# Expert weights of a mixture layer: experts taken one at a time, in longer runs, instead of two at a time

## What is computed

```python
# x: (1, 512, 1024); w_e1, w_e3: (16, 1024, 2816); w_e2: (16, 2816, 1024)
def _expert_choice_ffn(x, w_router, w_e1, w_e3, w_e2):
    cap = CAPACITY_FACTOR * n // N_EXPERTS                    # 64
    aff = jax.nn.softmax((x @ w_router).astype(F32), axis=-1)
    gate, idx = lax.top_k(jnp.swapaxes(aff, 1, 2), cap)
    xin = jax.vmap(lambda xb, ib: xb[ib])(x, idx)
    hid = jax.nn.silu(jnp.einsum('becd,edf->becf', xin, w_e1)) * jnp.einsum('becd,edf->becf', xin, w_e3)
    y = jnp.einsum('becf,efd->becd', hid, w_e2) * gate[..., None].astype(x.dtype)
    # y is added back at the token positions idx; then out = LN(alpha * h + sum)
```

## Time and profile before

| what | us |
|---|---|
| time, median of 3 runs | 2093.16 (2092.58 to 2097.62) |
| span of the profiled execution | 2092.3 |
| TensorE matmul busy | 1913.1 (91%) |
| VectorE, ScalarE, GpSimd busy | 649.0, 380.3, 252.2 |
| matmuls at L1078 idle on a transfer of expert weights | 102.1 |

### The profile page before, as it was taken

One profiled execution on the slowest core, in us unless ns is written; L12 is line 12 of the kernel. 1 busy time (PEld: TensorE's weight loads), 2 busy tenths in 40 slices (PEclk: granted clock), 3 DMA queues, 4 the chain that ended last, 5 costly groups with the idle time before them and its releaser, 6 DMA issues.

```text
span 2092.3 us, 20357 instructions
## 1 busy us (share of the span) xinstructions
PE 1913.1 (91%) x8502; PEld 954.8 (46%) x8502; DVE 649.0 (31%) x1149; ACT 380.3 (18%) x691; POOL 252.2 (12%) x268
## 2 busy tenths in 40 slices
PE   8989999999999997999798799898898888888897
PEld 4656554466678754343343343343343334334332
DVE  6599747588865442001001001001000000100102
ACT  1434313189810021000000000000000000000001
POOL 1786500065400000000000000000000000000001
PEclk9999999999999998999899999999999999999999
DMA  5631304143332576999999999999999999999995
GB/s 148 135 96 56 115 13 138 47 148 121 121 141 91 202 328 260 425 426 428 427 426 430 427 427 428 427 426 429 430 423 429 428 426 428 428 425 428 428 426 217
DMA packets 93786, 638.17 MB, mean 305 GB/s; under 512 B 21580, under 2 KB 35328, under 8 KB 62464
## 3 DMA queue, kind: packets, MB, share of 16 engines
q1 hardware_dynamic: 81056, 628.99, 74.0%
q10 hardware_dynamic: 12640, 7.89, 1.3%
HBM read 626.98 MB, written 9.88 MB: 304 GB/s over the span
## 4 chain that ended last, share of the span: by engine, by line
PE 59%; DMA 29%; DVE 2%; ACT 2%; issue 0%; SPq 0%; DVEq 0%
PE ps L1078 58%; DMA arena<-in_w_e 29%; ACT arena L730 1%; ACT L730 0%; PE ps L1189 0%; DVE arena L2191 0%; DVE arena L2148 0%; PE ps L1590 0%; SPq L531 0%; PE ps L1252 0%; PE ps L1306 0%; DVE arena L2185 0%; DVE arena L2092 0%; DVE arena L2094 0%; PE ps L1443 0%
## 5 line engine op out<-in xcount | busy, mean ns | idle before, releaser
L1078 PE MATMUL ps<-arena 128*64 128x512 f32 (+8 forms) x7968 | 1849.9, 515 | 144.4 <-DMA arena<-in_w_e 102.1
L1078 PEld LDWEIGHTS ps<-arena 128*64 128x64 f32 (+2 forms) x7968 | 893.7, 163 | 1077.7 <-issue 957.4
L730 ACT ACTIVATE arena<-ps 128x512 f32<-128x512 f32 (+6 forms) x288 | 155.8, 573 | 1591.2 <-PE ps L1078 903.8
L2157 DVE TENSOR_TENSOR arena<-arena,ps 128x512 f32<-128x512 f32 (+1 forms) x48 | 30.2, 643 | 575.3 <-PE ps L1078 575.3
L722 POOL TENSOR_TENSOR arena<-arena 128x1024 f32<-128x1024 f32 x3 | 7.0, 2349 | 1360.3 <-ACT arena L730 1360.3
L2166 DVE TENSOR_TENSOR arena<-arena,ps 128x512 f32<-128x512 f32 x48 | 33.1, 690 | 334.5 <-PE ps L1078 334.5
L730 ACT ACTIVATE arena<-arena 128x128 f32<-128x128 f32 (+10 forms) x261 | 117.7, 509 | 73.3 <-DVE arena L2116 19.1
L730 ACT ACT_TABLE_LOAD x74 | 94.9, 1283 | 25.5 <-issue 23.8
L1870 DVE SCALAR_TENSOR_TENSOR arena<-arena 128x512 f32<-128x512 f32 x80 | 63.5, 794 | 2.8
L2148 DVE TENSOR_TENSOR arena<-arena 128x512 f32<-128x512 f32 x8 | 5.5, 693 | 180.6 <-PE ps L1590 180.5
L682 POOL TENSOR_TENSOR arena<-arena 128x768 f32<-128x768 f32 x16 | 28.5, 1779 | 179.4 <-PE ps L1252 128.4
(11 more groups left out here) (206 smaller groups left out, 702.5 us busy)
## 6 DMA issues: line engine op xcount, KB each, us to landing
arena<-in_w_e SPq DMA_DIRECT2D x112, 2816.0 KB, 29.2
arena<-in_w_e SPq DMA_DIRECT2D x80, 2048.0 KB, 27.7
arena<-in_w_e SPq DMA_DIRECT2D x32, 1408.0 KB, 11.7
arena<-in_w_in SPq DMA_DIRECT2D x9, 2048.0 KB, 8.6
arena<-in_w_e SPq DMA_DIRECT2D x16, 1024.0 KB, 30.4
arena<-cumulative_scratch SPq DMA_DIRECT2D x16, 768.0 KB, 4.9
arena<-in_w_in SPq DMA_DIRECT2D x5, 1536.0 KB, 6.5
arena<-in_w_out_ssd SPq DMA_DIRECT2D x4, 1536.0 KB, 7.1
```

Source lines behind the costliest of these rows:

```text
L730: return act.activation(out, in_, func, **kw)
L1078: return pe.matmul(out, lhsT, rhs, start=a, stop=z)
L2157: tt(o, o, ps[:, i, 0:w], ALU.mult).then_inc(s.hid_ready, 1)
```

## The change

One expert is taken at a time. The two halves of the array now take the two halves of an expert's 2816 up columns (1408 each, in banks of 512, 512 and 384), and in `down` the two halves of its 1024 output columns; a matmul has the same shape of stationary operand as before. w_e1 accumulates in banks 0 to 2, w_e3 in banks 3 to 5, the output in bank 6. From expert 3 on each weight tensor of an expert comes as two pieces of 11,264 words per partition: four rows of w_e1 or w_e3, or eleven of w_e2, in one run of 45,056 bytes. Experts 0 to 2 and the last piece of expert 15 are cut finer. A piece's landing is told by one of 18 semaphores instead of 12. The loads of the second norm's rows are issued after the copy of expert 0's output. `gates_transposed`, `gather` and `sums_so_far` stand at other places between the products; the gathered columns of `h` are taken with a step of 4 instead of 2, the transposed blocks with a step of 11 instead of 4.

```diff
-BANKS = [(512 * i, min(512, FF - 512 * i)) for i in range(6)]
-ROW_BLOCKS = KT // 2
-BLOCKS = len(BANKS)
-LANDINGS = 12
-BY_ROWS = 2 * ROW_BLOCKS
+HALF_FF = FF // 2
+BANKS = [(512 * i, min(512, HALF_FF - 512 * i)) for i in range(3)]
+RUN = (4, 4, 11)
+ROW_WORDS = (FF, FF, D_MODEL)
+LANDINGS = 18
...
+def expert_pieces():
+    cuts = lambda x, w, j: {
+        (0, 0): [0, 1, 2, 3, 4], (0, 1): [0, 1, 2, 3, 4],
+        (0, 2): [0, 3, 5, 8, 11] if j == 0 else [0, 3, 6, 9, 11],
+        (1, 0): [0, 1, 2, 3, 4], (1, 1): [0, 2, 4], (1, 2): [0, 6, 11], (2, 0): [0, 2, 4], (2, 1): [0, 2, 4],
+        (EXPERTS - 1, 2): [0, 11] if j == 0 else [0, 6, 9, 11]}.get((x, w), [0, RUN[w]])
+    return [(x, w, j, r0, r1) for x in range(EXPERTS) for w in range(3) for j in range(2)
+            for r0, r1 in zip(cuts(x, w, j)[:-1], cuts(x, w, j)[1:])]
...
-        aside = {piece_at[0, 0]: hid_at, piece_at[ASIDE, 0]: aside_at, piece_at[ASIDE, 1]: aside_at + FF}
+        aside = {piece_of[0, 0, 1, 3]: hid_at, piece_of[0, 1, 1, 3]: aside_at, piece_of[0, 2, 0, 0]: aside_at + FF}
         piece_place, piece_behind = ring_places(piece_size, ring_at, WORDS, aside)
-        unit_landings = [sum(1 for v, e in pieces if v <= u and v % LANDINGS == u % LANDINGS) for u in range(len(unit_size))]
+        piece_landings = [i // LANDINGS + 1 for i in range(len(PIECES))]
...
+        piece_loaded = [sem(f"piece_loaded_{i}") for i in range(12)] + x_loaded + cum_loaded
+        landed_before = [0] * 12 + [1] * TT + [GROUPS * TT // 2] * 2
...
+        piece_released, n_used = [], 0
+        for x, w, j, r0, r1 in PIECES:
+            if j == 1 and r1 == RUN[w]:
+                piece_released.append((s.up_ps, 3 * (2 * x + w + 1)) if w < 2 else (s.y_ps, x + 1))
             else:
                 n_used += 1
-                unit_released += 2 * [(s.group_used, n_used)]
-
-        def landed(u):
-            return unit_loaded[u % LANDINGS], 16 * unit_landings[u]
+                piece_released.append((s.piece_used, n_used))
...
+            def load(i):
+                x, w, j, r0, r1 = PIECES[i]
+                n_ = RUN[w]
+                src = w_e[w][x][P * n_ * j:P * n_ * (j + 1)].rearrange("(p k) d -> p k d", k=n_)[:, r0:r1].rearrange("p k d -> p (k d)")
+                sp.dma_start(arena[:, piece_place[i]:piece_place[i] + piece_size[i]], src).then_inc(piece_loaded[i % LANDINGS], 16)
+
+            row = lambda w, k: piece_of[0, w, k // 4, k % 4]
+            early = [row(0, k) for k in range(7)] + [row(1, k) for k in range(4)]
+            late = [row(0, 7)] + [row(1, k) for k in (6, 5, 4, 7)] + [piece_of[0, 2, 0, 0]]
+            assert all(piece_place[i] + piece_size[i] <= W0 - router_words for i in early)
+            assert all(piece_behind[i] is None for i in early + late) and len(early + late) <= LANDINGS
+            assert piece_place[row(1, 6)] >= W0 + KT * 512
+            for i in early:
+                load(i)
             sp.wait_ge(s.mixT_ps, 2 * TT)
-            piece_loaded(0, 0)
+            load(row(0, 7))
             sp.wait_ge(s.wo_ps, 2 * TT - 1)
-            piece_loaded(8, 0)
+            load(row(1, 6))
             sp.wait_ge(s.wo_ps, 2 * TT)
-            piece_loaded(6, 1)
+            load(row(1, 5))
             sp.wait_ge(s.max_ready, TT)
-            piece_loaded(6, 0)
+            load(row(1, 4))
             sp.wait_ge(s.hT_ps, 2 * (TT - 1))
             sp.wait_ge(s.h_ready, TT - 1)
-            piece_loaded(ASIDE, 0)
+            load(row(1, 7))
             sp.wait_ge(s.h_ready, TT)
-            piece_loaded(ASIDE, 1)
-            for i, (u, e) in enumerate(pieces):
-                if (u, e) not in early + late:
-                    freed = [pieces[piece_behind[i]][0]] if piece_behind[i] is not None else []
-                    freed += [u - LANDINGS] if u >= LANDINGS else []
-                    sp.wait_ge(*unit_released[max(freed)])
-                    piece_loaded(u, e)
+            load(piece_of[0, 2, 0, 0])
+            for i in range(len(PIECES)):
+                if i not in early + late:
+                    freed = [piece_behind[i]] if piece_behind[i] is not None else []
+                    freed += [i - LANDINGS] if i >= LANDINGS else []
+                    if freed:
+                        sp.wait_ge(*piece_released[max(freed)])
+                    load(i)
...
+            def expert_rows(x):
+
+                e = x % 2
+                act.wait_ge(s.y_ps, x + 1)
+                if e == 0 and x:
+                    act.wait_ge(s.sc_ps, 2 * TT * (x // 2))
+                for n_ in range(2 if x + 1 < EXPERTS else 1):
+                    f(ye[64 * e:64 * e + 64, 512 * n_:512 * n_ + 512], ps[64 * n_:64 * n_ + 64, 6, :], ACT.Copy).then_inc(s.ye_copied, 1)
...
-                cols = [h[:, c, 256 * (kk // 2):256 * (kk // 2) + 256].rearrange("q (p t) -> q t p", t=2)[:, kk % 2, :] for c in range(TT)]
+                cols = [h[:, c, 512 * (kk // 4):512 * (kk // 4) + 512].rearrange("q (p t) -> q t p", t=4)[:, kk % 4, :] for c in range(TT)]
...
+            def up(x, which):
+                e = x % 2
+                for k in range(KT):
+                    w = weight_row(x, which, k // 4, k % 4)
+                    if x == 0 and which == 0:
+                        pe.wait_ge(s.xin_copied, k + 1)
+                    for i, (c0, n_) in enumerate(BANKS):
+                        for hf in range(2):
+                            at = HALF_FF * hf + c0
+                            r = mm(ps[64 * hf:64 * hf + 64, 3 * which + i, 0:n_], xin[:, k, 64 * e:64 * e + 64], w[:, at:at + n_], k == 0, k == KT - 1)
+                        if k == KT - 1:
+                            r.then_inc(s.up_ps, 1)
+                    row_used(r, x, which, k // 4, k % 4)
+                    if x == 0 and which == 0 and k + 2 < KT:
+                        first_gather(k + 2)
+                    if k == 3 and which == 0 and x and not e:
+                        scatter(x // 2 - 1)
+            def turn(x):
+                pe.wait_ge(s.hid_ready, 3 * (x + 1))
+                blocks = hid.rearrange("q (p t) -> q t p", t=RUN[2])
+                for t in range(RUN[2]):
+                    r = pe.transpose(ps[:, 3 + t // 4, P * (t % 4):P * (t % 4) + P], blocks[:, t, :], ident)
+                    if t % 4 == 3 or t == RUN[2] - 1:
+                        r.then_inc(s.hidT_ps, 1)
+            def down(x, j):
+                for t in range(RUN[2]):
+                    if j == 0 and t % 4 == 0:
+                        pe.wait_ge(s.hidT_copied, 3 * x + t // 4 + 1)
+                    w = weight_row(x, 2, j, t)
+                    for n_ in range(2):
+                        r = mm(ps[64 * n_:64 * n_ + 64, 6, :], hidT[:, t, 64 * j:64 * j + 64], w[:, 512 * n_:512 * n_ + 512],
+                               j == 0 and t == 0, j == 1 and t == RUN[2] - 1)
+                    row_used(r, x, 2, j, t)
+                if j == 1:
+                    r.then_inc(s.y_ps, 1)
...
+                if x and x % 2 == 0:
                     pe.wait_ge(s.xin_copied, KT + 2 * p)
-                    pe.wait_ge(s.selT_copied, p)
-                up(p, 0)
-                up(p, 1)
-                turn(p)
-                if p:
+                if x % 2:
+                    pe.wait_ge(s.selT_copied, p + 1)
+                up(x, 0)
+                pe.wait_ge(s.hidT_copied, 3 * x)
+                up(x, 1)
+                if x % 2 == 0:
+                    gates_transposed(p)
+                elif p + 1 < PAIRS:
+                    gather(p + 1, 0)
+                elif x % 2:
+                    pe.wait_ge(s.silu_half, 3 * EXPERTS)
+                    sums_so_far(0)
+                turn(x)
+                if x % 2 and p + 1 < PAIRS:
+                    gather(p + 1, 1)
+                if x % 2 == 0 and x:
                     pe.wait_ge(s.acc_added, 2 * TT * p)
-                down(p, range(3))
-                gates_transposed(p)
-                if p + 1 < PAIRS:
-                    gather(p + 1)
-                else:
-                    pe.wait_ge(s.hidT_copied, 6 * PAIRS)
-                    pe.wait_ge(s.selT_copied, PAIRS)
-                    for c in range(TT - 1):
+                elif x:
+                    pe.wait_ge(s.ye_copied, 2 * x)
+                down(x, 0)
+                if x == EXPERTS - 1:
+                    pe.wait_ge(s.hidT_copied, 3 * EXPERTS)
+                    for c in range(1, TT - 1):
                         sums_so_far(c)
-                down(p, range(3, BLOCKS))
-            pe.wait_ge(s.ye_copied, 2 * PAIRS)
+                down(x, 1)
+            pe.wait_ge(s.ye_copied, 2 * EXPERTS)
```

More of the change, by code:

```diff
@@ L164, in encoder @@
     SL = weight_slices()
-    GROUPS_E = expert_groups()
-    group_at = {g: i for i, g in enumerate(GROUPS_E)}
-    unit_size = [2 * FF if g[0] < 2 else BANKS[g[2]][1] // P * D_MODEL for g in GROUPS_E for e in range(2)]
+    PIECES = expert_pieces()
```

(54 more changed lines are left out.)

139 lines of the change are left out of this document (20 added, 119 removed).

## The result

The changed kernel takes 2098.14 us (median of 20 runs, 2094.58 to 2104.54), the kernel before 2095.08 (20 runs on the same chips, 2092.58 to 2097.77). The ratio is 1.0017, 95% interval 1.001 to 1.0023: 0.17% slower, inside the 0.3% that I called no change, and outside the range that I gave (2080 to 2096). On another chip the same two kernels gave 1.0019 (1.001 to 1.0029). I had forecast a gain of 7.5 us; the kernel lost 3 to 4.

A forecast was written before the change was run, and what follows sets the result against it. The experts were taken as bound by the rate at which weights arrive. Span 2092.3 - 10.8 (rate) + 0 (start) + 3.3 (end) = 2084.8, with 0.9 us outside 2085.6 us; range 2080 to 2096.

The forecast's parts named there:

- The rate: Weight transfers of the experts: longer runs raise GB/s to 431.8, saving 10.8 us in all.
- the line: Run time fitted through three measured lengths: 0.03676 ns a byte plus 13 ns per run, extrapolated to 45,056 bytes.
- Rival A: Weight transfers don't gain from the longer run (split, or memory sets the rate): 2094 or 2096.5 us, chance 0.18.
- The start: Stretch before transfers saturate, 803 to 926 us: as many bytes moved as before, 0 us, range -2 to +3.
- a gather step costs 1.3 us: First expert rows: 1.3 us per gather step plus 2.37 per row, so ring pieces are released each 3.67 us.
- the sign of being wrong: At the start of the experts: a loss of more than 3 us would show the forecast wrong.
- The queue never runs dry, with 8 to 9 us to spare: Ring of three weight pieces: TensorE always hands places back before the two queued pieces, 26.8 us of transfer, run out.
- where I had 29.5: Worst place, odd expert: first w_e2 piece used up 29.5 us after w_e3's second piece lands, half gathers counted 7.9 us.
- my limit of 38.7: Latest time for that hand-back: 13.4 + 26.8 - 1.5 = 38.7 us after the landing of w_e3's second piece.
- The end: Last expert: products end 9.1 us after the last byte, up to 1.6 more with a slow clock; +3.3 us taken.
- B (the clock): TensorE's clock drops with waits at each piece; below mean 0.82 TensorE decides, at 0.78 2135 us; chance 0.07.
- C: More gained: earlier first release helps the start, last-ending engines gain per run, end costs only 1: about 2079 us, chance 0.08.

The follow-up runs named there:

- contig_end_half: Changed kernel with h kept by row slices, last expert cut finer, and pieces of experts 3 to 15 cut in two: 2094.94 us, 0.9997 of the kernel before.
- contig_end: Changed kernel with h kept by row slices (gathers read at step 1) and last expert cut finer: 2088.48 us, 0.9964; on another chip 2090.25 us, 0.9971.
- step2_first: Changed kernel with the old step of 2 words in the first pair's eight gathers only (wrong columns, same work): 2093.37 us, 0.9990 of the kernel before.
- contig: Changed kernel with h kept by row slices, so gathers read with a step of 1 word and the norm is strided: 2090.53 us, 0.9974.
- step2: Changed kernel with all gathers reading h at the old step of 2 words (wrong columns, same work): 2089.24 us, 0.9972 of the kernel before.
- half: Changed kernel with every piece of experts 3 to 15 cut in two, seven ring places instead of three, step 4 kept: 2096.44 us, 1.0006.

## Why the prediction was wrong

**The rate: right.** -10.8 us from 13 ns a run. The row reads 432 where the line gives 431.8, and contig_end_half against contig_end shows the gain of a doubled run in the time, 4.7 to 6.5 us for the line's 7.7. Rival A is out.

**The start: wrong, and it is the step "a gather step costs 1.3 us".** I took the cost of `first_gather` from rows of the kernel before and carried it over, although the change reads `h` with another step. I priced the step for the transposes only, where going from 4 to 11 words costs next to nothing (216 ns a load at step 11, 211 at step 4), and so never asked it of the gathers. It costs 0.9 us for eight instructions; 6 rows are 5.5 us, and step2_first gives 4.8 back. With it the start lost twice the 3 us that I had set as the sign of being wrong. Without it the start is as forecast: 377 GB/s against 382, 1.4 us, inside my -2 to +3.
The groups that hold the gathers' weight loads show a mean of 191 ns with step 1, 196 with step 2 and 301 with step 4, and the 32 loads of half a gather take 3.65, 3.89 and 7.54 us (contig, step2, the changed kernel). The Trainium skill (Advanced Engine Details and Errata, "SBUF Cachelines") has the rule: lines of 16 bytes, at least two hits on a line to hide the latency. Four words are 16 bytes, one hit a line; two words are two hits. The gathers agree with it. The transposes, at 211 ns for 4 words and 216 for 11, are slower than at step 1 (141), but eleven of them go through in 1.5 us, 0.14 us each against a gather's 0.24, which the rule doesn't account for and no run here settles. I had named the steps in describing the change and didn't hold them against this rule.

**"The queue never runs dry, with 8 to 9 us to spare": wrong, by two terms of that sum.** The 7.5 us of the gather, and the spread of the engines. Expert 5's case: the second piece of w_e3 is in at 1231.8; the chain, start and us:

```profile
1231.82 19.04 PE ps L1074 x80
...
1250.86 1.33 PE ps L1546 x11
```

And SyncE's timeline, the issue that waited for the first piece of w_e2 to be used up:

```profile
1269.28 0.33 SPq L524 DMA_DIRECT2D arena<-in_w_e  x1
```

37.5 us after the landing, where I had 29.5; 7.5 of the 8.0 more are the gather. That is still before my limit of 38.7, and yet from 1265 to 1270 the transfers were at 0.52. Nearly all of that loss lies in its last 3 us:

```profile
1267.00:1270.00 3.00, 3.00 (x18) 0.99 (x16) 0.00 (x0) 0.00 (x0) 0.00 (x0) 1.00 0.25 105
```

By the trace's packets all 16 engines are at work at 1267, eight at 1268, three at 1269.5 and one at 1270. My limit counts from landings, which come with the slowest engine, while the others run out of work up to 3 us sooner. The earlier trace rows had shown such a spread, half of the engines done 8 us before the last, and I used that row for the end and not for the queue. With the gather at its old length (step2) no such stretch is left, and with seven places in the ring (half) none is left either, so the loss takes the long gather and the three places together: 4.1 us by the runs, 4.2 by the shares of the three stretches. That the spread turned the last 1.2 us of slack into a loss is read from the trace; no run varies the spread.

**The end: right in kind, 0.8 us short.** By the chain the last copy begins 4.06 us later than before (2077.21 against 2073.15), with the last byte near 2066 in both, for a forecast of 3.3. Two terms were off and partly cancel. Before the change the products end at 2073.1 and not at 2072.1, since the copy at 2073.15 waits for them:

```profile
2073.15 0.69 DVE L2180 COPY arena<-ps 128x512 f32<-128x512 f32 x1 [47.65 <-PE ps L1078]
```

So they ended 7.1 us behind the last byte, not 6.1. And now they end some 11 us behind it (2077.2 against 2066), where I had 9.1 to 10.5. The first stretch of the end took 13.30 us for 52 instructions: 2.2 more than 9.4 + 1.7, the slow clock that I had at 1.6 (granted clock 0.88 from 2039 to 2053).

**The sum.** 2092.3 - 10.8 + 0 + 3.3. In the profiled execution 6.0 us are lost by 925, 4.8 in the middle (429 GB/s where step2 has 431, over 1040 us; both are rounded to 1 GB/s, so 2.4 either way), and the end costs 4.1: 2092.3 - 10.8 + 6.0 + 4.8 + 4.1 = 2096.4, the span. That it meets to the tenth is chance, by that rounding. With the step put back, step2 stands 6.5 us below the kernel before on its chip, and the forecast was 7.5.

**The rivals.** B (the clock) didn't happen: the granted clock is 0.96 over the middle, not below 0.82. (Its sum of the work of a pair adds up to 132.9 us, not 131, which would put the limit at 0.83.) C didn't either. None of them had the gather, and the range with its 10 us above the forecast had no term for it.

## What to carry to other kernels

When a layout is changed so that transfers get longer runs, list every on-chip reader of the data whose row order must follow, with its step before and after: here the loads that pay for it sit in another operand than the one that was moved. Take the slack of a queue from its fastest engine and not from the landing that the consumer waits for: here the first ran dry up to 3 us before the last. And a run-length line through three measured lengths held here at twice the longest, so such an extrapolation may be priced with its line.

## What the runs showed of the hardware

- One contiguous run on one transfer engine takes 13 ns and 0.0368 ns a byte from 11,264 up to 45,056 bytes: 422, 426, 428.5 and 432 GB/s on 16 engines.
- A 128-column float32 weight load and its matmul, back to back in a gather: a gather of 64 takes 7.6 us with a step of 1 word, 7.9 with 2 and 15.4 with 4.
- VectorE pays for a step as well: 512 elements take 1.08 to 1.10 us with the output at a step of 128 words and 1.11 to 1.14 us with an input at a step of 4, against 1.28 us for 1024 without a step.
